# An intermediate copy in SBUF for a head pair's attention result, and later waits of the compression beside it

## What is computed

```python
o_a = banded_attention(q_a, k_a, v_a, tbl[:, :8], WINDOW_A, sinks_a)        # 8 heads, window 128, sinks
kv_c = compress_kv(kv_b[:, :, 0:2], cmp_pos, cmp_w1, cmp_b1, cmp_w2, cmp_b2) # 31 compressed keys
k_c = rms_norm(kv_c[0], k_norm_b); v_c = kv_c[1]
o_cmp, o_sel = nsa_cmp_sel(q_b, k_c, v_c, k_s, v_s, tbl_b)                   # 8 heads
o_win = banded_attention(q_b, k_w, v_w, tbl_b, WINDOW_B, None)
o_b = gates[:, :, 0] * o_cmp + gates[:, :, 1] * o_sel + gates[:, :, 2] * o_win
x = x + concatenate([o_a, o_b]) @ w_mix_out
```

## Time and profile before

| | us |
|---|---|
| median of 3 runs | 2224.39 (2224.09 to 2224.95) |
| the profiled execution's own time | 2223.66 |
| its span in the trace | 2222.1 |
| TensorE busy | 2176.4 (98%) |
| VectorE busy | 1275.6 (57%) |
| ScalarE busy | 898.9 (40%) |
| GpSimd busy | 267.4 (12%) |

### The profile page before, as it was taken

How to read it: one execution, slowest core, us unless ns; L and a number is a source line. 1 busy time by engine, 2 the same in 40 slices (tenths; PEclk the granted TensorE clock), 3 DMA queues, 4 the chain that set the end, 5 groups by cost and what they waited for, 6 DMA issues and landing times.

```text
span 2222.1 us, 30869 instructions
## 1 busy us (share of the span) xinstructions
PE 2176.4 (98%) x11681; PEld 1816.4 (82%) x11681; DVE 1275.6 (57%) x2136; ACT 898.9 (40%) x1492; POOL 267.4 (12%) x445
## 2 busy tenths in 40 slices
PE   7999999998999999999999999999999999999998
PEld 6888888877888888888888888888878788888887
DVE  5764764557753363365347766456476766555654
ACT  4222223456642222225237544234264745432343
POOL 2110220045300020010027000000000430000000
PEclk9999999999999999999999999999999999999999
DMA  8864993231034284274231342332313112323332
GB/s 263 285 207 125 320 304 103 95 88 39 30 114 114 76 273 142 66 246 143 95 105 41 91 110 79 105 100 80 114 50 102 61 48 80 100 86 104 94 93 96
DMA packets 260212, 270.42 MB, mean 122 GB/s; under 512 B 9190, under 2 KB 202365, under 8 KB 260109
## 3 DMA queue, kind: packets, MB, share of 16 engines
q1 hardware_dynamic: 238381, 190.40, 28.8%
q0 software_dynamic: 21728, 78.63, 10.2%
HBM read 265.72 MB, written 12.72 MB: 125 GB/s over the span
## 4 chain that ended last, share of the span: by engine, by line
PE 85%; DVE 6%; ACT 5%; issue 1%; POOL 1%; DMA 1%; SPq 0%; DVEq 0%; ACTq 0%; POOLq 0%
PE bank L345 16%; PE bank L346 16%; PE bank L347 15%; PE bank L351 11%; PE bank L353 11%; PE bank L352 11%; PE bank L1857 2%; PE bank L1832 2%; PE bank L1810 2%; ACT probs L1906 1%; DVE w_lo L328 1%; ACT w_hi L324 1%; POOL probs L2032 1%; DVE probs L1974 1%; ACT xT_hi L773 1%
## 5 line engine op out<-in xcount | busy, mean ns | idle before, releaser
L345 PE MATMUL bank<-xT_hi,w_hi 128*128 128x512 f32 (+1 forms) x1624 | 620.3, 382 | 7.0 <-DVE xT_lo L789 2.3
L346 PE MATMUL bank<-xT_lo,w_hi 128*128 128x512 f32 (+1 forms) x1624 | 618.3, 381 | 0.0
L347 PE MATMUL bank<-xT_hi,w_lo 128*128 128x512 f32 (+1 forms) x1624 | 618.2, 381 | 0.0
L328 DVE TENSOR_TENSOR w_lo<-raw,w_hi 128x2048 fp32r<-128x2048 f32 (+2 forms) x200 | 411.0, 2055 | 316.8 <-ACT w_hi L324 315.1
L324 ACT ACTIVATE w_hi<-raw 128x2048 fp32r<-128x2048 f32 (+3 forms) x201 | 345.9, 1721 | 453.5 <-PE bank L353 396.2
L345 PEld LDWEIGHTS bank<-xT_hi,w_hi 128*128 128x128 f32 x1624 | 304.6, 188 | 69.1 <-DVE w_lo L328 5.4
L347 PEld LDWEIGHTS bank<-xT_hi,w_lo 128*128 128x128 f32 x1624 | 304.6, 188 | 59.2
L346 PEld LDWEIGHTS bank<-xT_lo,w_hi 128*128 128x128 f32 x1624 | 304.6, 188 | 58.0
L351 PE MATMUL bank<-w_hi,hid_hi 128*128 128x512 f32 x704 | 274.1, 389 | 0.0
L353 PE MATMUL bank<-w_hi,hid_lo 128*128 128x512 f32 x704 | 273.9, 389 | 0.0
L352 PE MATMUL bank<-w_lo,hid_hi 128*128 128x512 f32 x704 | 273.9, 389 | 0.0
(11 more groups left out here) (330 smaller groups left out, 2754.6 us busy)
## 6 DMA issues: line engine op xcount, KB each, us to landing
raw<-in_ffn_w_in_dram SPq DMA_DIRECT2D x40, 1024.0 KB, 6.2
raw<-in_f_win_dram SPq DMA_DIRECT2D x40, 1024.0 KB, 6.0
mod_w<-in_mod_w_dram POOLq DMA_DIRECT2D x48, 512.0 KB, 5.9
mod_w_more<-in_mod_w_dram POOLq DMA_DIRECT2D x48, 512.0 KB, 6.1
raw<-in_ffn_w_out_dram SPq DMA_DIRECT2D x24, 768.0 KB, 4.6
raw<-in_f_wout_dram SPq DMA_DIRECT2D x24, 768.0 KB, 4.5
raw<-in_a_wqkv_dram SPq DMA_DIRECT2D x12, 1024.0 KB, 5.1
skewed_strips<-bias_strips POOLq DMA_DIRECT2D x32, 320.0 KB, 6.8
```

The source lines that it names most:

```text
L328: dve.tensor_tensor(out=w_lo[:, slot, :n], in0=raw[:, slot, :n], in1=w_hi[:, slot, :n].bitcast(f32), op=ALU.subtract).then_inc(lo_done, 1)
L345: pe.matmul(o, lhsT=w[0], rhs=xs[0], start=first, stop=False)
L346: pe.matmul(o, lhsT=w[0], rhs=xs[1], start=False, stop=False)
L347: return pe.matmul(o, lhsT=w[1], rhs=xs[0], start=False, stop=last)
```

## The change

For `att_1` alone a buffer `out` is given (`cT[:, 0, :]`). ScalarE then copies bank 7 to `out` (first waiting, from the second group on, until the lo of the group before has been made), signals that, waits for its own signal, and writes hi from `out`. VectorE makes lo from `out` instead of the bank. TensorE's first values of the next group wait for the copy, not for lo. The other attentions keep the old way.

The compression's second layer, its bias and square go from iteration 6 to 7, the compressed values of VectorE too; mean and square root go from 8 to 9; TensorE's wait for the square root and VectorE's normalized keys from 9 to 10. TensorE's wait for the projection's last lo half goes from iteration 2 to 3, in front of the gates' transposes.

```diff
-            def __init__(self, groups, probs, hi, lo, lag=1, places=None):
+            def __init__(self, groups, probs, hi, lo, lag=1, places=None, out=None):
...
+                self.lag, self.out = lag, out
+                self.out_copied = sem("pair_out")
...
                 if k in self.first and k:
-                    pe.wait_ge(self.l, self.g0 + self.first[k])
+                    if self.out is None:
+                        pe.wait_ge(self.l, self.g0 + self.first[k])
+                    else:
+                        pe.wait_ge(self.out_copied, self.first[k])
...
                 act.wait_ge(self.o, self.after("o", k))
-                act.activation(self.hi[:, self.last[k], :], bank[7][:, :], ACT.Copy).then_inc(self.h, 1)
+                if self.out is None:
+                    act.activation(self.hi[:, self.last[k], :], bank[7][:, :], ACT.Copy).then_inc(self.h, 1)
+                    return
+                g = self.last[k]
+                if g:
+                    act.wait_ge(self.l, self.g0 + g)
+                act.activation(self.out, bank[7][:, :], ACT.Copy).then_inc(self.out_copied, 1)
+                act.wait_ge(self.out_copied, g + 1)
+                act.activation(self.hi[:, g, :], self.out, ACT.Copy).then_inc(self.h, 1)
...
-                dve.tensor_tensor(out=self.lo[:, g, :], in0=bank[7][:, :], in1=self.hi[:, g, :].bitcast(f32),
+                dve.tensor_tensor(out=self.lo[:, g, :], in0=bank[7][:, :] if self.out is None else self.out, in1=self.hi[:, g, :].bitcast(f32),
...
-                              probs_0, q0_hi, q0_lo, 2, probs_0_at)
+                              probs_0, q0_hi, q0_lo, 2, probs_0_at, cT[:, 0, :])
...
-        cmp_pe = {1: lambda pe: proj.between_scores_pe(pe), 2: lambda pe: pe.wait_ge(p_out, 4 * TOK), 3: lambda pe: proj.gates_T_pe(pe), 4: pre_pe, 6: cmp_out_pe, 8: cmp_mean_pe,
-                  9: lambda pe: pe.wait_ge(c_sd, 1)}
+        def gates_T_pe(pe):
+            pe.wait_ge(p_out, 4 * TOK)
+            proj.gates_T_pe(pe)
+
+        cmp_pe = {1: lambda pe: proj.between_scores_pe(pe), 3: gates_T_pe, 4: pre_pe, 7: cmp_out_pe, 9: cmp_mean_pe,
+                  10: lambda pe: pe.wait_ge(c_sd, 1)}
...
-                   4: gates_and_hid_act, 6: cmp_sq_act, 8: cmp_sd_act, 13: lambda act: next_hi(act, proj.gates_c)}
-        cmp_dve = {0: lambda dve: dve.wait_ge(p_gk, 1), 3: lambda dve: proj.gates_dve(dve), 4: gates_and_in_dve, 5: cmp_hid_dve, 9: cmp_k_dve}
+                   4: gates_and_hid_act, 7: cmp_sq_act, 9: cmp_sd_act, 13: lambda act: next_hi(act, proj.gates_c)}
+        cmp_dve = {0: lambda dve: dve.wait_ge(p_gk, 1), 3: lambda dve: proj.gates_dve(dve), 4: gates_and_in_dve, 5: cmp_hid_dve, 10: cmp_k_dve}
...
-                                    6: cmp_v_dve,
+                                    7: cmp_v_dve,
```

More of the change, by code:

```diff
@@ L1717, in program @@
         class PairAttention:
-            def __init__(self, groups, probs, hi, lo, lag=1, places=None):
+            def __init__(self, groups, probs, hi, lo, lag=1, places=None, out=None):
                 self.groups, self.probs, self.hi, self.lo = groups, probs, hi, lo
-                self.lag = lag
+                self.lag, self.out = lag, out
+                self.out_copied = sem("pair_out")
                 self.places = places or (lambda k: range(3 * (k % (lag + 1)), 3 * (k % (lag + 1)) + 3))
```

## The result

The changed kernel takes 2231.01 us (median of 13 runs, 2229.28 to 2235.43), the kernel before beside it 2224.64 (median of 13, 2222.73 to 2226.72). The ratio is 1.003, with a 95% interval of 1.0023 to 1.0037: slower by 6.4 us, between 5.1 and 8.2. The forecast was 2230.0, slower by 5.65.

A forecast was written before the change was run, and what follows sets the result against it. ScalarE and VectorE were taken to bound the first attention, TensorE's waits being spare. 3.04 us up to k = 10 and 11, 1.95 for mixed groups and 0.66 for the last made 5.65: 2230.0 us, range 2226.2 to 2233.0.

The forecast's parts named there:

- What bounds the kernel: First attention: VectorE and ScalarE hold up the work; TensorE's waits, 4.4 us of them for lo, are mostly spare time.
- A = 0.66: ScalarE's extra time per pair of heads: 0.10 lost overlap, 0.03 gap, 0.53 slot; bounds 0.53 to 0.78 us.
- Copies of the banded groups: Pair copies at k = 4, 6, 8, where ScalarE runs without a break: 0.66 us each, 1.98 us.
- cmp_v at k = 7: VectorE's compressed values moved from k = 6 to 7: 0.35 us gained, 0.45 lost, net +0.10 us.
- Square root and keys: Table loads moved to k = 9, keys' normalization (1.33 us) to k = 10: k = 10 starts 2.90 us late, 0.82 from these moves.
- k = 10 and 11: TensorE's values wait for ScalarE's score copy behind the new hi copy: +3.04 us so far; lateness beyond that is hidden.
- Mixed groups and the last pair: Hi copy ahead of exponentials at k = 15, 20, 25: 0.65 us each, 1.95; ahead of the next weights' split: 0.66.
- p_out, c_hid: TensorE's moved waits on p_out (0.8 us) and c_hid (1.1 us): edits with no price, other waits taking their place.
- The faster rival: Bank 7 bounds the banded stretch, so TensorE's 6.3 us of waits vanish: -3.7 us, 2220.7 us; chance 0.08.
- The sum: Whole kernel: 3.04 + 1.95 + 0.66 = 5.65 us slower, 2230.0 us; bounds of the copy's price make it 4.6 to 6.6.
- The rival of 0.18: TensorE's clock falls to 1.2 GHz after idle pieces up to 540.5: +2.2 us more, 2232.2 us; chance 0.18.

The follow-up runs named there:

- copy_only: Changed kernel with only the pair's copy through SBUF; compression steps and p_out wait at their old places: 2228.74 us against 2223.96 before, ratio 1.0019.
- act_time: Kernel before plus one unread ScalarE copy behind each of the 8 hi copies; TensorE still waits for lo: 2228.18 us, ratio 1.0020 to before.
- moves_only: Changed kernel without the buffer: compression steps and p_out wait moved, hi and lo made from the bank: 2226.35 us against 2223.96 before, ratio 1.0015.
- filler: Changed kernel with TensorE's scores of k = 9, 10 and 11 made twice into the same banks: 2230.01 us against 2224.89 before, ratio 1.0021.
- k_norm_at_8: Kernel before with only the keys' normalization moved behind the bias of k = 8: 2224.48 us, ratio 0.9995 to before.
- banded_only: Changed kernel, but mixed pairs (groups 4 to 7) make hi and lo from the bank, TensorE waiting for lo: 2228.49 us against 2224.89 before, ratio 1.0021.

## Why the prediction was right

**What bounds the kernel.** Right. TensorE's waits in this stage were spare time; taking away those on lo gave about 0.3 us by the delays (copy_only against act_time).

**A = 0.66.** Right, with its parts (gap 0.03, 0.60 between the starts, 0.54 to the next).

**Copies of the banded groups.** Right: 0.65 at k = 5, 0.66 more at k = 9 of copy_only. At k = 7 0.97 was forecast and 0.98 measured. In copy_only, where cmp_v stays at k = 6, the copy of that iteration costs 0.32 just as well: the 0.35 by which cmp_v held VectorE there covers the rest.

**cmp_v at k = 7.** Forecast 1.42 at k = 8, measured 1.52: the term of +0.10 was 0.20.

**Square root and keys.** Forecast -0.65 at k = 9 and +2.90 at k = 10; measured -0.54 and +3.13. Of the 0.23, 0.10 came in from k = 8. The keys' normalization was taken at 1.33 us "at either place"; it lasted from 534.04 to 535.55, 1.51, and nearly all of the difference is its CAST, 0.44 where it was 0.25. That goes with the place: the CAST takes 0.44 or 0.45 in all five traces with the keys at k = 10, with the copies or without (moves_only), 0.25 or 0.26 in the five with them at k = 9, and 0.20 in the three with them at k = 8. In each of the 13 traces it ends 0.04 to 0.08 us behind an instruction of GpSimd. At k = 10 that one scales 256 columns twice (1.10 us), at k = 9 128 columns twice (0.91 us). So most likely GpSimd's work holds it up; no run took that work away. By kernels: copies alone come to 0.66 + 0.31 + 0.66 = 1.63 at k = 10 by the forecast's method, so the moves were to add 2.90 - 1.63 = 1.27; measured are 1.65 (copy_only) and 3.12 - 1.65 = 1.47.

**k = 10 and 11.** The values were to start 3.04 late; 539.47 + 1.23 - 537.46 = 3.24. TensorE then was to run unbroken and hide what lay beyond 3.04: in filler the delay settles at 3.40, from 3.77 at k = 11. The copy at k = 10, taken at 0.14, cost 0.28 (3.12 to 3.40 in filler, 1.65 to 1.93 in copy_only).

**Mixed groups and the last pair.** Forecast 0.65 each and 0.66, 2.61 together; measured 2.68. Waits of 1.33 and of 2.58 as expected.

**p_out, c_hid.** Right at nothing. From the scores of k = 0 to the compression it takes 14.96 us before and 14.98 after, and TensorE waits 0.63 for a bias where it had waited for p_out.

**The faster rival's point.** It was to decide if TensorE's scores of k = 10 came after VectorE was ready for them. They were nearer to that than the 0.2 us of the earlier trace rows let one think: k_norm_at_8 shows 0.14 us. But the copy and the moves make VectorE later, not earlier, and so the point wasn't reached.

**The sum.** 5.65 forecast; 3.40 + 2.65 = 6.05 at full clock, and 6.4 in the medians. The price of the slot in the Trainium skill, page "ScalarE: Activation LUTs", section "What ACT_TABLE_LOAD costs", would have made A 0.61, as an estimate from its figures. The rows have 0.66: the one copy held ScalarE for 0.48 us where those figures give 0.52, the pair for 1.14 where they give 1.13. The measurement decides.

**The clock.** The rival of 0.18 did come, in three of 18 executions: two are traced, the third is told by its mean clock. TensorE idled up to 540 and was then the bound, as told, but such idle pieces aren't enough to bring the fall at that place: banded_only has them too, and no fall at k = 11. Its size was not as told: 2.2 us was the price of twenty values and ten transposes, and the clock stayed at 0.50 for 13 us of unbroken work, 5.4 us. The median is, by its mean clock, an execution without the fall, and so it came within 1 us of a sum that leaves the fall out. The Trainium skill, page "TensorE: Matmul & The Clock Gate", Part 1, ties the two levels to how busy the engine has been; by that rule the traces agree, in that the clock fell behind pieces in which TensorE idled, though not behind each of them.

## What to carry to other kernels

Before shortening what an engine waits for, read whether the waits of its consumers name it: TensorE waited 4.4 us for lo, but VectorE waited 0.2 us for TensorE, so a release that cost ScalarE 0.66 us per pair had next to nothing to gain. A table load or a fixed piece beside a pipeline is priced by the slack of the iteration in which it stands, so look for the iteration where its reader waits anyway, and check that the engine freed by it isn't held by the next one. When a change adds idle time to TensorE just before a stretch that TensorE bounds, price that whole stretch at 1.2 GHz as a risk, not its first instructions.

## What the runs showed of the hardware

- The clock fell at k = 11 in the two profiled executions of the changed kernel after a stretch of many short waits, none over 1.9 us, with TensorE busy 0.57 to 1.6 of each two microseconds from 526 to 540. By their mean clocks, it didn't fall there in 15 of 18 executions of the same kernel. banded_only, with the same work up to there, had its clock low for about 4 us at k = 10 instead and full at k = 11.
- The scores of three steps made twice in TensorE's waits moved no delay up to k = 11 by more than 0.02 us. The clock was 1.00 from 524 to 556 in that one trace.
- A kernel with less delay can have its low clock elsewhere, with no effect: copy_only has 0.50 to 0.56 from 528 to 534, where its twelve values take 1.55 us, and its delay at k = 10 stays at 1.65, as TensorE isn't the bound there.
- A CAST of 128x64 on VectorE from SBUF to SBUF took 0.20, 0.25 or 0.44 us, by what GpSimd did beside it: it ended 0.04 to 0.08 us behind GpSimd's instruction in all 13 traces.
